# A sparse-expert layer: 160 instead of 128 tokens taken row by row, and a third of the low halves on another engine

## The reference, cut to what matters

```python
def peer_ffn(h, w_query, sub_keys, u_tab, v_tab):
    ...                       # scores, two top-16, best 16 of 256 sums
    gates = jax.nn.softmax(best_s, axis=-1)
    def one_block(args):
        h_blk, i_blk, g_blk = args
        u_sel = u_tab[i_blk]
        act = jax.nn.gelu(jnp.einsum('td,thkd->thk', h_blk, u_sel).astype(jnp.float32))
        w = (g_blk * act).astype(h.dtype)
        return jnp.einsum('thk,thkd->td', w, v_tab[i_blk])
```

## Time and profile before

| | |
|---|---|
| median of 3 runs | 3061.89 us (3061.42 to 3063.77) |
| the profiled execution, its own time | 3085.22 us |
| its span, first to last instruction | 3083.4 us |
| TensorE busy | 2993.4 us, 97% |
| VectorE, ScalarE, GpSimd busy | 2037.5, 1228.6, 745.1 us |
| V stage on TensorE, first to last matmul | 2512.6 to 3079.8 us |

### The profile page before, as it was taken

The page is one execution under the profiler, slowest core; times in us unless marked ns, Lnnn a source line. Parts: engine busy times, 40 slices in busy tenths (PEclk is TensorE's granted clock), DMA queues, the critical chain, the costliest instruction groups (busy, mean ns, idle before and its releaser), DMA issues.

```text
span 3083.4 us, 37566 instructions
## 1 busy us (share of the span) xinstructions
PE 2993.4 (97%) x13961; PEld 2466.0 (80%) x13961; DVE 2037.5 (66%) x3402; ACT 1228.6 (40%) x2166; POOL 745.1 (24%) x443
## 2 busy tenths in 40 slices
PE   8999999999999989999999999999999988999999
PEld 7877787877877756676677888888888878999999
DVE  6678534447798889934754589767770026878887
ACT  4266232224323332122533323399992222333332
POOL 0000000003304000000000244433334454656651
PEclk9999999999999999999999999999999998999999
DMA  6156435554354455433113244456767466999996
GB/s 219 51 194 215 143 114 204 191 174 171 122 192 156 156 209 168 145 116 123 48 55 96 88 131 143 138 169 182 219 191 222 140 227 224 346 361 349 348 368 218
DMA packets 310391, 564.92 MB, mean 183 GB/s; under 512 B 124344, under 2 KB 164408, under 8 KB 309824
## 3 DMA queue, kind: packets, MB, share of 16 engines
q1 hardware_dynamic: 185376, 460.18, 43.6%
q0 software_dynamic: 22528, 67.19, 5.7%
q10 hardware_dynamic: 102304, 35.13, 4.4%
HBM read 489.51 MB, written 139.98 MB: 204 GB/s over the span
## 4 chain that ended last, share of the span: by engine, by line
PE 88%; DVE 7%; issue 2%; ACT 2%; DMA 1%; POOL 0%; SPq 0%; ACTq 0%; DVEq 0%
PE psum L669 88%; DVE wl L1528 1%; ACT wh L1107 1%; DVE yb L1740 0%; DVE psum L1904 0%; DVE trig L1623 0%; DMA xc<-xc 0%; DVE trig L1626 0%; DVE lb L1731 0%; DVE trig L1628 0%; DVE trig L1625 0%; DVE trigw L1627 0%; DVE trigw L1624 0%; DVE st L1981 0%; DVE cs L1738 0%
## 5 line engine op out<-in xcount | busy, mean ns | idle before, releaser
L669 PE MATMUL psum<-h_hi,wh 128*128 128x512 f32 x2144 | 856.9, 400 | 31.2 <-DVE h_lo L1672 13.2
L669 PE MATMUL psum<-h_hi,wl 128*128 128x512 f32 x2144 | 849.6, 396 | 0.0
L2306 POOL TENSOR_TENSOR wl<-ring,wh 128x1024 fp32r<-128x1024 f32 x170 | 422.7, 2487 | 1766.3 <-ACT wh L1107 1766.3
L669 PE MATMUL psum<-h_lo,wh 128*128 128x512 f32 x2144 | 849.2, 396 | 0.0
L1107 ACT ACTIVATE wh<-ring 128x1024 fp32r<-128x1024 f32 (+2 forms) x492 | 504.5, 1028 | 603.6 <-PE psum L669 505.3
L1528 DVE TENSOR_TENSOR wl<-ring,wh 128x1024 fp32r<-128x1024 f32 (+2 forms) x322 | 375.8, 1171 | 519.4 <-ACT wh L1107 467.8
L669 PEld LDWEIGHTS psum<-h_hi,wh 128*128 128x128 f32 x2144 | 406.3, 190 | 133.1 <-issue 39.5
L669 PEld LDWEIGHTS psum<-h_hi,wl 128*128 128x128 f32 x2144 | 405.5, 189 | 95.5
L669 PEld LDWEIGHTS psum<-h_lo,wh 128*128 128x128 f32 x2144 | 406.2, 189 | 89.6 <-issue 1.7
L669 PE MATMUL psum<-ews_hi,wh 128*128 128x384 f32 x1024 | 349.8, 342 | 14.1 <-DVE wl L1528 8.3
L669 PE MATMUL psum<-ews_lo,wh 128*128 128x384 f32 x1024 | 349.3, 341 | 3.7 <-issue 3.7
(11 more groups left out here) (398 smaller groups left out, 4135.2 us busy)
## 6 DMA issues: line engine op xcount, KB each, us to landing
ring<-tables SPq DMA_DIRECT2D x256, 512.0 KB
rows_scratch<-tables SPq DMA_DIRECT2D x128, 512.0 KB, 5.0
acts_scratch<-ga SPq DMA_DIRECT2D x128, 256.0 KB, 2.2
gates_scratch<-stage ACTq DMA_DIRECT2D x6, 4096.0 KB, 21.5
abuf<-acts_scratch SPq DMA_DIRECT2D x128, 192.0 KB
gbuf<-gates_scratch SPq DMA_DIRECT2D x128, 192.0 KB
ring<-w_up SPq DMA_DIRECT2D x44, 512.0 KB
ring<-w_modb SPq DMA_DIRECT2D x32, 512.0 KB
```

Source lines behind the costliest of these rows:

```text
L669: return nc.tensor.matmul(out, lhsT, rhs, start=first, stop=last, **kw)
L2306: g.tensor_tensor(wl, slot(WHOLE_OF[e], 0, D), wh.bitcast(F32), ALU.subtract)\
```

## The change

The row-by-row tokens become 160 (SPT = 128 + SX, SX = 32), the dense ones TD = 352. The 32 new tokens have 128 picks each; they are packed in 32 more picks, each of which serves four groups of 32 partitions: partition 32 q + t has pick q of four for token t. They have an accumulator of their own, and a matmul with `sel` (four stacked identities) adds the four groups. There are NPICK = 160 picks; every fifth is a packed one.

The activations of the sparse tokens are stored behind the V rows: `rows_scratch` has rows of RW = 1184 numbers, of which the last 160 are written in the U stage by a second store of each tile. So a picked row brings its activations along, and the single-activation picks go. `share` takes the right one out by a product with the identity (or with `sel`) that is summed into `share_of` by an accumulator.

NV_ROWS becomes 12, LAG 5, the gates are parked in eight groups of 44 tokens and not six of 64. `high_of_gated` of the first four tiles moves into ScalarE's U loop, and TensorE's wait for the last activation moves from ahead of V tile 0 to V tile 1. The low halves of V tiles 1, 4, 7, ... go from VectorE to GpSimd (`VO_BY_GP`), which makes them in between its picks.

```diff
+SX = 32
+SPT = P + SX
+TD = T - SPT
+TG = 44
+RW = D + SPT
+NV_ROWS = 12
...
+LAG = 5
+NPICK = PK + SX
+PACKED = [a for a in range(NPICK) if SX and a % (NPICK // SX) == NPICK // SX - 1]
+COLUMN = [P + PACKED.index(a) if a in PACKED else a - sum(p < a for p in PACKED) for a in range(NPICK)]
+ADDED_AT = [-(-(a + 1) * (PK - LAG - 2) // NPICK) + LAG - 1 for a in range(NPICK)]
+VO_BY_GP = [v for v in range(PK) if v % 3 == 1]
...
                 sp.wait_ge(S("ea_ready"), j + 1)
-                sp.dma_start(acts_d[j], ga4[:, j % 4, :]).then_inc(S(f"act_parked{j % 4}"), 16)
+                sp.dma_start(acts_d[j], ga4[:, j % 4, 0:TD]).then_inc(S(f"act_parked{j % 4}"), 16)
+                sp.dma_start(rows_d[j * P:(j + 1) * P, D:RW], ga4[:, j % 4, TD:T])\
+                    .then_inc(S(f"act_parked{j % 4}"), 16)
+                if j == 60 and SX:
+                    sp.wait_ge(S("picks_ready"), NB + 1)
+                    for q in range(P // SX):
+                        at = slice(q * SX, (q + 1) * SX)
+                        sp.dma_start(wanted[at, :, P:NPICK], unpacked[P - SX:P, :, at]).then_inc(S("once_loaded"), 16)
...
                 halves_here(pe, e)
+                if v == 1:
+                    pe.wait_ge(S("ea_ready"), PK)
...
-                        last = nc.tensor.transpose(psum[:, dc, TD:T], accs[:, 0, dc * P:(dc + 1) * P], ident[:, :])
+                        mm(psum[:, dc, TD:TD + SX], accs[:, 2, dc * P:(dc + 1) * P], sel, True, True)
+                        last = nc.tensor.transpose(psum[:, dc, TD + SX:T], accs[:, 0, dc * P:(dc + 1) * P],
+                                                   ident[:, :])
...
-            pe.wait_ge(S("ea_ready"), PK)
...
+                if PK - 16 <= j < PK - 12:
+                    high_of_gated(j - (PK - 16))
...
             def rest_half(k):
-                low(HALF[TILE[f"vo{k}"]])
+                if k not in VO_BY_GP:
+                    low(HALF[TILE[f"vo{k}"]])
+
+            def share(a):
+                c = COLUMN[a]
+                ve.wait_ge(S(f"rows_loaded{a // 2 % (NV_ROWS // 2)}"),
+                           32 * (a // NV_ROWS + 1))
+                wait(ve, S("share_made"), a - 1)
+                if c < P:
+                    acts, one = vrow[a % NV_ROWS][:, D + SX:RW], ident[:, :]
                 else:
+                    acts, one = vrow[a % NV_ROWS][:, D:D + SX], sel
+                STT(junk[:, a % 2, 0:acts.shape[1]], acts, gate_s[:, c:c + 1], one, ALU.mult, ALU.mult,
+                    accum_out=share_of[:, c:c + 1]).then_inc(S("share_made"), 1)
+
+            def add_row(a):
+                c = COLUMN[a]
+                acc, by = accs[:, 2 if c >= P else c % 2, :], share_of[:, c:c + 1]
+                ve.wait_ge(S("share_made"), a + 1)
+                if c in (0, 1, P):
+                    ins = TS(acc, vrow[a % NV_ROWS][:, 0:D], by, None, ALU.mult)
+                else:
+                    ve.wait_ge(S("rows_summed"), a - 1)
+                    ins = STT(acc, vrow[a % NV_ROWS][:, 0:D], by, acc, ALU.mult, ALU.add)
                 ins.then_inc(S("rows_summed"), 1)
...
+                while added < NPICK and ADDED_AT[added] <= k:
+                    if added == 0:
+                        share(0)
+                    if added + 1 < NPICK:
+                        share(added + 1)
                     add_row(added)
...
+            def pick(a):
+                c = COLUMN[a]
+                if a >= NV_ROWS and a % 2 == 0:
+                    gp.wait_ge(S("rows_summed"), a - NV_ROWS + 2)
+                g.indirect_dma_start(out=vrow[a % NV_ROWS], out_offset=None, in_=rows_d,
+                                     in_offset=bass.IndirectOffsetOnAxis(ap=row_of[:, c:c + 1], axis=0))\
+                    .then_inc(S(f"rows_loaded{a // 2 % (NV_ROWS // 2)}"), 16)
...
             for j in range(PK):
                 low(f"ui{j}")
+            for v in VO_BY_GP:
+                if v < RH:
+                    low(f"vo{v}")
             gp.wait_ge(S("picks_ready"), NB + 1)
+            gp.wait_ge(S("once_loaded"), ONCE["packed"])
...
             for k in range(4):
+                gp.wait_ge(S(f"act_parked{k}"), 32 * (PK // 4))
+            a = 0
+            for v in range(RH, PK):
+                while a < NPICK and (a < NV_ROWS or ADDED_AT[a - NV_ROWS + 1 - a % 2] < v - 3):
+                    pick(a)
+                    a += 1
+                if v in VO_BY_GP:
+                    low(f"vo{v}")
```

More of the change, by code:

```diff
@@ L232 @@
             if _split:
-                _sem = "low_by_gp" if _name.startswith("ui") or _name in FFN_BY_GP else "low_by_ve"
+                _by_gp = _name[:2] == "ui" or _name in FFN_BY_GP or _name[:2] == "vo" and int(_name[2:]) in VO_BY_GP
+                _sem = "low_by_gp" if _by_gp else "low_by_ve"
                 _lows[_sem] = _lows.get(_sem, 0) + 1
@@ L405, in build @@
         ews, er = both("ews", B + 2 * NV * TD, NV, TD), ar("er", B + 4 * NV * TD, 2, TD)
[L407 to L412, removed]
+        accs = ar("accs", 4096, 4, D)
+        share_of, junk = ar("share_of", B + 10000, 1, NPICK)[:, 0, :], ar("junk", B + 10176, 2, P)
+        vrow = [ar(f"vrow{k}", at, 1, RW)[:, 0, :] for k, at in
+                enumerate([B + 10496 + RW * k for k in range(NV_ROWS - 1)] + [8192])]
+        wanted = ar("wanted", B + 26640, 2, NPICK)
+        row_of, gate_s = wanted[:, 0, :].bitcast(U32), wanted[:, 1, :]
+        sel, unpacked = ar("sel", B + 26960, 1, 32)[:, 0, :], ar("unpacked", B + 26992, 2, P)
         silu = ar("silu", B + 26000, KD, 2 * MA)
@@ L426, in build @@
         one_col = sm(2 * HEADS - 1)
-        token = sm(1)
         epsc, silu_c = V("eps"), sm(KD)
@@ L2258, in _ @@
                     rest_of_gated(k + 4)
-                while added < PK and (added + 1) * (PK - LAG - 2) <= (k + 1 - LAG) * PK:
+                while added < NPICK and ADDED_AT[added] <= k:
[3 more added lines that the diff above has]
+                        share(added + 1)
                     add_row(added)
                     added += 1
-            assert added == PK
-            ve.wait_ge(S("rows_summed"), PK)
+            assert added == NPICK
+            ve.wait_ge(S("rows_summed"), NPICK)
             TT(accs[:, 0, :], accs[:, 0, :], accs[:, 1, :], ALU.add).then_inc(S("rows_summed"), 1)
@@ L2337, in _ @@
                 gp.wait_ge(S(f"gates_parked{k}"), 16 * (TD // TG // 2))
-            for k in range(NV_ROWS):
-                pick_row(k)
             for k in range(4):
-                gp.wait_ge(S(f"act_parked{k}"), 16 * (PK // 4))
-            for n in range(2):
-                pick_acts(n)
-            for k in range(NV_ROWS, PK):
-                if k % PICK_GROUP == 0 and k // PICK_GROUP + 1 < PK // PICK_GROUP:
-                    pick_acts(k // PICK_GROUP + 1)
-                pick_row(k)
+                gp.wait_ge(S(f"act_parked{k}"), 32 * (PK // 4))
[6 more added lines that the diff above has]
+                    low(f"vo{v}")
+            while a < NPICK:
+                pick(a)
+                a += 1
 HEAD_SCALE = float(P) ** -0.5
```

72 lines of the change are left out of this document (20 added, 52 removed).

## The result

The changed kernel takes 3143.4 us (median of 4 runs, 3140.1 to 3149.7) beside 3062.6 for the one before: ratio 1.0262, 95% interval 1.0249 to 1.0275. It is slower, by 81 us, where 12 less were forecast. Of the 93 us between forecast and result, some 53 are lost ahead of the V stage by a step that was costed at nothing, some 27 lie in the way from the profiled execution to the median, and 12 in the V stage.

A forecast was written before the change was run, and what follows sets the result against it. VectorE, held by the port it shares with GpSimd, becomes the bound: 2534 + 526 = 3060 us for its last sum, span 3071.8 against 3083.4; scaled to the median, 3061.9 - 11.5 = 3050 us, range 3000 to 3078.

The forecast's parts named there:

- the DMA, picks and the rest: V stage: DMA 4.1 us a tile, GpSimd 3.2, under VectorE's 4.4; extra stores and eight parkings hidden under the U stage.
- the two stretches: V stage, 2541 to 2562.5 and 2754 to 2763.5: TensorE slow, 15.4 and 4.8 us lost, counted as gone with single-activation picks.
- The second rival: The slow TensorE stretches are the profiled execution's own, so the timed runs never had them: 3050 + 20 = 3070; chance 0.18.
- VectorE with the port is the bound: V stage: 442 us of VectorE's own work plus 84 of waiting for GpSimd make 526 us, 4.4 us a tile.
- The hold: V stage: each low half moved to GpSimd holds VectorE for 2.1 us; 40 x 2.1 = 84 us, bounds 0 and 96.
- GpSimd's low halves well over 2.41 us: V stage: a sign to look for, GpSimd's low halves lengthened, with VectorE's instructions beside them 1 to 2 us longer.
- The share: V stage: 160 new scalar_tensor_tensors with an accumulator, 0.37 us wide, 0.1 less narrow; 56 us, bounds 40 and 72.
- The gap ahead of V4: Start of V stage: TensorE waits 7 us for V4's low half behind GpSimd's twelve picks, replacing the 8.3 us gap.
- the sum: End of V stage: 2534 + 526 = 3060 for VectorE's last sum, plus 11.8 us: span 3071.8 against 3083.4.
- Narrower matmuls: V stage: 352 columns instead of 384 take 161.3 ns, not 175.4; 43 us less if TensorE stays the bound.
- this rival: V stage: the port does not bind, GpSimd's low halves fall where VectorE waits anyway; median 2990 to 3012, chance 0.22.
- Slower by the share: V stage: the accumulator's read costs VectorE as much as ScalarE's or more, from 0.48 us a share on; chance 0.18.

The follow-up runs named there:

- the parkings cured: The changed kernel with gates parked in 11 groups of 32 tokens in place of 8 groups of 44: 3086.3 us, 1.0072 times the kernel before.
- the kernel without the third: The changed kernel with all low halves of the V tiles on VectorE again, none on GpSimd: 3078.9 us, 1.0047 times the kernel before.

## Why the prediction was wrong, point by point

- **The step that failed** is in the part on the DMA, picks and the rest: "eight parkings of gates in place of six ... lie under TensorE's U stage". They cost 53 us, in the part of the kernel of which the prediction says at its start that the change touches almost nothing there. The landing before (21.5 us) would have fitted into the 35.5 us of a smaller group too; what the step didn't weigh is that the time of the transfer changes with where its pieces start and end: 41.3 us for 2816 KB, where 4096 KB took 21.5. Nor did "if that cover were gone, each would cost its own issue or step once" hold: the cost is a wait of VectorE's for a staging buffer, once a group.
- **From the profiled execution to the median.** The span forecast, 3071.8, already left out the two stretches; the scaling to the median took 21.8 us off again, most of the 23.3 us by which that execution, with its stretches, stood above the median. (The change's median is 5.1 us over its span: 26.9 in all.) The second rival had this right: 3050 + 20 = 3070. With that, and the parkings cured, the measured 3086 is 16 over it, 12 of them in the V stage, below.
- **VectorE with the port is the bound:** right, and by nearly the time said. From first V matmul to the end of the span 571.2 us were forecast, 583.0 to 583.6 measured; that it is so near is in part luck. In the kernel with parkings of 32, VectorE's first share starts at 2537.5 (forecast 2534), behind a wait of 8.1 us for gates while the DMA moves 418 GB/s (2525 to 2535); its last sum ends at 3069.6, 532 us later (forecast 526), and 15.2 us follow (11.8). Inside the stream two sizes were off, 17 us too little and 16 too much, and cancel. *The hold:* against the kernel without the third, 84 x (1825 - 1218) + 157 x (1532 - 1286) + 123 x (603 - 521) + 128 x (357 - 345) ns = 101 us for 43 low halves, 2.35 each and not 2.1; nearly the whole of GpSimd's 2.45 us. The sign "GpSimd's low halves well over 2.41 us" did not come: the hold falls on VectorE, whose low half took 3.94 us beside one of 2.38. *The share:* 0.27 us from its start to the next instruction's (2537.47 to 2537.74), 0.17 for narrow ones, 40 us and not 56. The accumulator is read by an instruction of its own, as the Trainium skill says in VectorE: DVE Perf Modes, section "Two Vector instructions with no wait between them"; the trace agrees that there are two, but the read takes 77 ns and lies under the next, so the upper bound that the prediction set beside that sentence was the wrong one.
- **The gap ahead of V4** was forecast as 7 us with picks from 2505.5 and the low half's end at 2523. With parkings of 32 it is 7.14 us and ends at 2524.5. That V0 has no gap was right too. But the sum takes VectorE's start, and with it the end, from this gap, and that is not borne out: counted from the first V matmul, an earlier low half of V4 brought the first share 9.6 us forward and the end 2.7.
- **Narrower matmuls** gave what was said where TensorE was free: 21 in a row start at 2554.73 to 2557.91 in the changed kernel, 159 ns apart; 161 was forecast.
- **The rivals.** The port does bind: without the third the V stage is 41 us shorter. The time that this rival gave is wrong even without a port: VectorE alone at 96% and the DMA at 411 GB/s leave a span of 3044, not 3020 to 3035. Slower by the share: no, a share costs 0.27 us and not 0.48.

## What to carry to other kernels

A transfer's size in bytes doesn't say what it costs: when an edit changes how long a stored piece is or where it starts, cost the transfer anew, against the time in which its buffer is wanted back. A low half that moves to GpSimd while VectorE reads two SBUF tensors holds VectorE for longer (2.35 us) than it frees it (1.14): with 12% idle time on VectorE TensorE stayed full, on a full VectorE the move cost 41 us. VectorE, TensorE and the DMA, all near their limits, are balanced by the size of the split (144 tokens here), and a profiled execution far above the median has to be explained before differences are taken from it.

## What the runs showed of the hardware

- Stores to DRAM in 16384 pieces of 128 bytes: 19.3 us on multiples of 128, 26.9 shifted by 32 or 64, 55 to 57 shifted by 16. The Trainium skill, DMA: Bandwidth & Descriptors, section Specifications, gives 512 bytes as the least for full rate and says that smaller ones are read, modified and written; that sentence does not tell 128, 176 and 256 bytes apart, nor a piece from a shifted one, and the table does. The Trainium skill, Collectives: The Full Stack, section "Rules for kernel authors", asks for buffers aligned to 32 bytes, to prevent a read-modify-write; it is written for collectives, and the step from 26.9 to 56.6 us in these plain stores agrees, though the reads themselves are in no row here.
- A scalar_tensor_tensor of VectorE's with an accumulator is followed by a read of 77 to 83 ns, where ScalarE's takes 201.
- In the V stage of the two kernels of 160 tokens without the third, where VectorE waits 34 us for gates, the DMA stands at 404 to 412 GB/s from 2600 to 3000, near the fullest slices of before.
- Beside a low half of GpSimd's of 2.38 us, VectorE's low half (two SBUF inputs) takes 3.94 us in place of 1.21.
